# The prompt's attention output computed by token instead of by feature, in a fused prompt and decode step

## The reference, cut to what matters

```
qkv = rms_norm(x) @ w_in                                  # prompt and sample
A) 4 heads, two 64-wide components, 128-wide values:
     w  = softmax(q1 k1^T) - lam * softmax(q2 k2^T)       # causal
     oa = rms_norm(w @ v, subln_g) * (1 - lambda_init)    # norm over each head's 128 values
B) 8 heads x 64, masked softmax:  ob = softmax(q k^T + mask) @ v
x = x + concat(oa, ob) @ w_out
x = x + (silu(h @ w_gate) * (h @ w_up)) @ w_down,  h = rms_norm(x, norm_ffn_g)
y = rms_norm(x, norm_final_g)
```

## Time and profile before

| | |
|---|---|
| median of 3 runs | 1169.67 us (1168.24 to 1173.23) |
| the profiled execution: its own time, its span | 1171.82 us, 1169.7 us |
| mean granted TensorE clock, as a share of full speed | 0.942 |
| busy: PE, PEld, DVE, ACT, POOL | 995.5, 879.7, 568.2, 419.3, 250.3 us |
| attention pieces e0 to e71 | about 332 to 532 us |
| output projection of the prompt | about 535 to 645 us |
| norm and last slots of the sample | about 645 to 742 us |
| feed-forward, final norm | from 742 us |

### The profile page before, as it was taken

The page is one execution under the profiler, slowest core; times in us unless marked ns, Lnnn a source line. Parts: engine busy times, 40 slices in busy tenths (PEclk is TensorE's granted clock), DMA queues, the critical chain, the costliest instruction groups (busy, mean ns, idle before and its releaser), DMA issues.

```text
span 1169.7 us, 29082 instructions
## 1 busy us (share of the span) xinstructions
PE 995.5 (85%) x11290; PEld 879.7 (75%) x11290; DVE 568.2 (49%) x1367; ACT 419.3 (36%) x908; POOL 250.3 (21%) x107
## 2 busy tenths in 40 slices
PE   3978898988878868676887576899999999999994
PEld 3967887777655546454666454899999999999994
DVE  4479747876368999962445252322322322200003
ACT  5553543363126555653413331222222222212112
POOL 2212121211000010102110001333433334433330
PEclk8989999999888998988999788999999999999997
DMA  8589999999899999688986995477676776865632
GB/s 265 209 257 301 327 316 361 361 330 344 308 334 345 350 364 311 211 265 272 318 274 203 265 294 162 164 266 250 233 264 224 263 266 253 296 205 184 217 121 81
DMA packets 202415, 310.90 MB, mean 266 GB/s; under 512 B 14465, under 2 KB 111106, under 8 KB 200770
## 3 DMA queue, kind: packets, MB, share of 16 engines
q1 hardware_dynamic: 200386, 305.24, 77.7%
q10 hardware_dynamic: 1920, 4.20, 1.3%
HBM read 302.30 MB, written 73.92 MB: 322 GB/s over the span
## 4 chain that ended last, share of the span: by engine, by line
PE 51%; DVE 14%; SPq 13%; DMA 10%; issue 7%; ACT 5%; DVEq 0%; ACTq 0%
PE ps L1216 35%; SPq L547 7%; PE ps L897 5%; DMA v_ring<-in_cache_v_diff 4%; DVE kt_sb L1806 3%; SPq L627 3%; PE ps L1085 3%; PE ps L1123 3%; DMA c_raw<-in_w_up 2%; ACT q_st L1476 1%; DVE sub_r L1781 1%; DMA v_ring<-in_state_v_win 1%; DMA g_ffn<-in_norm_ffn_g 1%; DMA k_ring<-in_state_k_win 1%; PE ps L1043 1%
## 5 line engine op out<-in xcount | busy, mean ns | idle before, releaser
L1806 DVE STREAM_TRANSPOSE kt_sb<-k_ring 128x512 f32<-128x512 f32 x336 | 217.5, 686 | 76.7 <-PE ps L1085 31.6
L842 POOL TENSOR_TENSOR c_lo<-c_raw,c_hi 128x1024 fp32r<-128x1024 f32 (+1 forms) x60 | 157.0, 2616 | 364.5 <-ACT c_hi L1529 356.4
L1529 ACT ACTIVATE c_hi<-c_raw 128x1024 fp32r<-128x1024 f32 (+1 forms) x60 | 68.8, 1146 | 316.0 <-PE ps L1216 268.0
L1216 PE MATMUL ps<-h_hi,c_lo 128*128 128x288 f32 x672 | 144.2, 295 | 0.0
L1216 PE MATMUL ps<-h_hi,c_hi 128*128 128x288 f32 x672 | 143.1, 293 | 0.9 <-DVE ffn_tmp L1988 0.9
L1123 PE MATMUL ps<-v_ring,pt_sb 128*32 128x128 f32 (+1 forms) x2496 | 94.0, 296 | 58.0 <-DMA v_ring<-in_cache_v_diff 41.2
L1216 PE MATMUL ps<-h_lo,c_hi 128*128 128x288 f32 x672 | 142.1, 293 | 0.0
L897 PE MATMUL ps<-h_hi,w_hi 128*128 128x288 f32 x384 | 126.1, 328 | 4.4 <-DVE h_lo L1675 2.3
L1123 PEld LDWEIGHTS ps<-v_ring,pt_sb 128*32 128x32 f32 (+1 forms) x2496 | 72.7, 118 | 73.6 <-issue 63.9
L897 PE MATMUL ps<-h_lo,w_hi 128*128 128x288 f32 x384 | 115.7, 301 | 0.0
L897 PE MATMUL ps<-h_hi,w_lo 128*128 128x288 f32 x384 | 115.4, 301 | 0.0
(11 more groups left out here) (172 smaller groups left out, 1587.2 us busy)
## 6 DMA issues: line engine op xcount, KB each, us to landing
k_ring<-in_cache_k_diff SPq DMA_DIRECT2D x256, 256.0 KB, 5.1
v_ring<-in_cache_v_diff SPq DMA_DIRECT2D x256, 256.0 KB, 5.2
out_k_win_sample<-in_state_k_win SPq DMA_DIRECT2D x32, 1020.0 KB, 7.5
out_v_win_sample<-in_state_v_win SPq DMA_DIRECT2D x32, 1020.0 KB, 7.8
k_ring<-in_state_k_win SPq DMA_DIRECT2D x80, 256.0 KB, 5.8
w_raw<-in_w_in SPq DMA_DIRECT2D x24, 512.0 KB, 6.2
c_raw<-in_w_gate SPq DMA_DIRECT2D x22, 512.0 KB, 3.8
c_raw<-in_w_up SPq DMA_DIRECT2D x22, 512.0 KB, 4.2
```

The costliest lines, as they stand in the source:

```text
L842: nc.gpsimd.tensor_tensor(c_lo[:, j, 0:width], c_raw[:, j, 0:width], c_hi[:, j, 0:width].bitcast(F32), ALU.subtract).then_inc(w_lo_done, 1)
L1216: last = nc.tensor.matmul(main_ps[:, 2 * bank + c, 0:HALF], wt[:, j, w], act[:, k0 + k, c * HALF:(c + 1) * HALF], start=start and k == 0 a ...
L1529: nc.scalar.activation(c_hi[:, j, 0:width], c_raw[:, j, 0:width], ACT.Copy).then_inc(w_hi_done, 1)
L1806: V.transpose(kt_sb[:, i, :], k_ring[:, i, :]).then_inc(kt_done, 1)
```

## The change

1. **Output by token.** `weigh` swaps operands: the turned probabilities are the stationary side and the values the moving side, so Y has queries on partitions. For T from 4 each of the two heads moves 64 columns where 128 moved before.
2. **Inverse sums as columns.** For T from 4 the probabilities are no longer scaled: both L1731 instructions go, PE's `turn_weights` waits for ACT's exponentials alone, and DVE's new `evac_out` multiplies Y by the inverse sums (a step-0 operand) while it copies. ACT keeps the copy for T below 4.
3. **Head norm as columns.** The sums of squares are now over the free axis: ACT takes them 128 columns at a time into `head_r` (128x4 a head), DVE's means and inversions and ACT's roots are on 128x4, in three groups (heads 0 and 1, head 2, head 3) where the roots were in two. POOL scales `oT` in four pieces a head, once. The matrix-of-ones products of the prompt go.
4. **Turned back.** PE turns each head's four blocks into bank X (`turn_head`) at e36, e41, ..., e71, after the sample's uses of that step. `mix` reads X one and two pieces later on ACT (which applies g_sub8 for T below 4) and DVE; DVE's part frees X. The output projection takes the tiles in plain order.
5. **Loads.** `g_ffn` has another place and is loaded at o8 (slot 37) after the fourth head's squares. The first chunks of gate and up are issued at slot 45 step 1 instead of slot 48. ACT waits for `scored` before the norm's first squares.

```diff
-        if has_v(t):
-            out.append(("p", t))
...
+            for p in pieces(t, i):
+                if p < OUT and p - ATTN in TURN_AT:
+                    out.append(("h", TURN_AT.index(p - ATTN)))
...
-SQUARES_AT = (19, 27, 35, 43)
-ROOT_AT = (31, 47)
-INVERT_AT = (32, 34, 36, 38, 48, 50, 52, 54)
-HEAD_SCALE_AT = (37, 41, 53, 57)
-MIX_AT = {40: 0, 44: 1, 47: 4, 55: 5, 56: 2, 60: 3, 63: 6, 71: 7}
+SQUARES_AT = (16, 24, 32, 40)
+MEAN_AT, ROOT_AT, INVERT_AT = (27, 36, 43), (29, 38, 45), (31, 40, 47)
+NORMED = ((0, 2), (2, 3), (3, 4))
+HEAD_SCALE_AT = (33, 34, 42, 49)
+TURN_AT = (36, 41, 46, 51, 56, 61, 66, 71)
...
+                if p == OUT + 8:
+                    sp.wait_ge(sub_sq_done, 4)
+                    sp.dma_start(g_ffn[:, :], ins["norm_ffn_g"].partition_broadcast(P)).then_inc(norm_in[1], 16)
...
-                    if (t, i) == (KSLOTS, 1):
-                        sp.wait_ge(scored, KSLOTS)
-                        sp.dma_start(g_ffn[:, :], ins["norm_ffn_g"].partition_broadcast(P)).then_inc(norm_in[1], 16)
-                    if (t, i) == (KSLOTS + 4, 1):
+                    if (t, i) == (KSLOTS + 1, 1):
                         sp.wait_ge(e_t, KT)
                         c_chunk(C_GU, 0, KT, w_gate[:, :, 0:P])
                         c_chunk(C_GU + 1, 1, KT, w_up[:, :, 0:P])
...
             def head_scale(g):
-                r = sub_r[g // 2][:, g % 2, :]
-                pool.wait_ge(sub_rstd, 2 * g + 2)
-                nc.gpsimd.tensor_tensor(r, r, oT[:, g, :], ALU.mult).then_inc(sub_rstd2, 1)
-                pool.wait_ge(sub_rstd2, g + 1)
-                nc.gpsimd.tensor_scalar(oT[:, g, :], r, g_sub8, None, ALU.mult).then_inc(sub_norm, 1)
+                pool.wait_ge(sub_rstd, g + 1)
+                for blk in range(4):
+                    o = oT[:, g, blk * P:(blk + 1) * P]
+                    last = nc.gpsimd.tensor_scalar(o, o, head_r[g][:, blk:blk + 1], None, ALU.mult)
+                last.then_inc(sub_norm, 1)
...
-                pe.wait_ge(weights, u + 1)
+                if u < 16:
+                    pe.wait_ge(weights, u + 1)
+                else:
+                    pe.wait_ge(probs, u + 1)
...
+                        weights_t = probT[:, u % 2, c, kb * P:(kb + 1) * P]
                         if T >= 4:
-                            r = slice(64 * c, 64 * c + 64)
-                            dst, w = Y[r, cols], v_tok[:, kb, T * P + 64 * c:T * P + 64 * c + 64]
+                            last = nc.tensor.matmul(Y[:, qb * P + 64 * c:qb * P + 64 * c + 64], weights_t,
+                                                    v_tok[:, kb, T * P + 64 * c:T * P + 64 * c + 64],
+                                                    start=kb == 0, stop=kb == qb)
...
-            def sum_squares(g):
...
-                nc.tensor.matmul(Z[1], ones[:, :], sub_sq[:, g % 2, :], start=True, stop=True).then_inc(z_full[1], 1)
+            def turn_head(g):
+                if g < 4:
+                    pe.wait_ge(sub_norm, g + 1)
+                else:
+                    pe.wait_ge(y_free, Y_NO["a", g] + 1)
+                pe.wait_ge(x_free, X_NO["h", g])
+                for blk in range(4):
+                    last = nc.tensor.transpose(X[:, blk * P:(blk + 1) * P], oT[:, g, blk * P:(blk + 1) * P], ident[:, :])
+                last.then_inc(x_full, 1)
...
+            def head_squares(g):
+                act.wait_ge(y_free, Y_NO["a", g] + 1)
...
+                for blk in range(4):
+                    last = nc.scalar.activation(head_junk[:, blk, :], oT[:, g, blk * P:(blk + 1) * P], ACT.Square,
+                                                accum_out=head_r[g][:, blk:blk + 1])
...
-                nc.scalar.activation(mix_h[:, g, :], oT[:, g, :], ACT.Copy).then_inc(mix_hi, 1)
+                act.wait_ge(x_full, X_NO["h", g] + 1)
+                nc.scalar.activation(mix_h[:, g, :], X, ACT.Copy, scale=g_sub8 if g < 4 else 1.0).then_inc(mix_hi, 1)
...
+            def evac_out(T):          # on DVE, T from 4
+                dve.wait_ge(pv_done, 4 * T + 4)
+                dve.wait_ge(prd_done, 4 * T + 4)
+                V.tensor_tensor(oT[:, T, :].rearrange("p (k i) -> p k i", i=64), Y.rearrange("p (k i) -> p k i", i=64),
+                                prd[T % 2].unsqueeze(2).to_broadcast([P, 8, 64]), ALU.mult).then_inc(y_free, 1)
...
+            def head_mean(w):
+                for g in range(*NORMED[w]):
+                    dve.wait_ge(sub_sq_done, g + 1)
+                    V.tensor_scalar(head_r[g], head_r[g], 1.0 / P, SUB_EPS, ALU.mult, ALU.add).then_inc(sub_mean, 1)
...
                     if e in INVERT_AT:
-                        w = INVERT_AT.index(e)
-                        r = sub_r[w // 4][:, w // 2 % 2, w % 2 * (SEQ // 2):w % 2 * (SEQ // 2) + SEQ // 2]
-                        dve.wait_ge(sub_rms, w // 4 + 1)
-                        V.reciprocal(r, r).then_inc(sub_rstd, 1)
+                        for g in range(*NORMED[INVERT_AT.index(e)]):
+                            dve.wait_ge(sub_rms, g + 1)
+                            V.reciprocal(head_r[g], head_r[g]).then_inc(sub_rstd, 1)
```

More of the change, by code:

```diff
@@ L220, in x_order @@
     for t in range(SLOTS):
-        if has_v(t):
-            out.append(("p", t))
-        if has_v(t) and is_last(t - LAG):
-            out.append(("m", t))
-        if has_v(t - 1) and is_last(t - 1 - LAG):
-            out.append(("o", item_of(t - 1 - LAG)[0]))
+        for i in range(8):
+            if i == 4 and has_v(t):
+                out.append(("p", t))
+            if i == 6 and has_v(t) and is_last(t - LAG):
+                out.append(("m", t))
+            if i == 6 and has_v(t - 1) and is_last(t - 1 - LAG):
+                out.append(("o", item_of(t - 1 - LAG)[0]))
+            for p in pieces(t, i):
+                if p < OUT and p - ATTN in TURN_AT:
+                    out.append(("h", TURN_AT.index(p - ATTN)))
     return {what: k for k, what in enumerate(out)}
@@ L403, in build @@
         q_st = at("q_st", [P, 2, 4, 4, 32], Q1)
-        g_ffn = at("g_ffn", [P, D], Q1)
+        sq_junk2 = at("sq_junk2", [P, D], Q1)
         q_nat = at("q_nat", [P, 4, 32], region(512))
@@ L441, in build @@
         pden = small[:, 206:214]
[L442 removed]
+        prd = [small[:, 214:222], small[:, 351:359]]
         wide = small[:, 222:254]
@@ L1035, in out_tile @@
                         pe.wait_ge(masked, UNITS)
[L1036 to L1037 removed]
+                for k in (2 * kk, 2 * kk + 1):
                     w = slice(k * P, k * P + P)
                     if m == 0:
[L1040 removed]
+                        pe.wait_ge(x_free, X_NO["h", k] + 1)
                     for wt, act, at_first in ((o_hi[m % 2][:, w], mix_h, True), (o_hi[m % 2][:, w], mix_l, False),
                                               (o_lo[:, m % 2, w], mix_h, False)):
[L1043 to L1044 removed]
+                        last = nc.tensor.matmul(M[m % 2], wt, act[:, k, :], start=k == 0 and at_first,
+                                                stop=k == KT - 1 and act is mix_h and not at_first)
                 if kk == 3:
@@ L1399, in main @@
                         act.wait_ge(e_added, KT)
+                        act.wait_ge(scored, KSLOTS)
                     if r % 2 == 0 and r < 8:
@@ L1409, in main @@
                     m, kk = divmod(p - OUT, 4)
+                    if p == OUT:
+                        mix(KT - 1)
                     if m < KT - 1 and kk == 0:
@@ L1762, in main @@
                     m, kk = divmod(p - OUT, 4)
-                    if p == OUT:
-                        mix(MIXED[-1])
+                    if p == OUT + 1:
+                        mix(KT - 1)
                     if kk == 0 and 2 <= m:
```

101 lines of the change are left out of this document (42 added, 59 removed).

## The result

The changed kernel takes 1164.13 us (median, 1158.21 to 1172.61, 20 runs) where the kernel before, run beside it, took 1171.82 (1166.15 to 1181.72, 20 runs). The ratio is 0.9929, 95% interval [0.9904, 0.9953]: 8.3 us faster, 5.5 to 11.2. The profiled execution took 1161.06 us (span 1159.1), so profile against profile it is 10.8 us. Forecast were 16.5.

A forecast was written before the change was run, and what follows sets the result against it. DVE and DMA were taken as full from 376 to 430, DVE alone to 489, PE from 742. Terms -9 + 0.5 - 8 = -16.5 us from 1171.82 gave 1155.3 (median terms 1153), own range 1149 to 1158, 8 in 10 within 1143 to 1166.

The forecast's parts named there:

- the 8 us of the end: Last slots: early gate and up chunks end ACT's stand and PE's 9.44 us wait, so slot 51 starts 8 us sooner.
- the 9 of the attention: Whole attention: -8 us from 430 to 489, -2 from 489 to 530, +1 for bank X, together -9 us.
- Attention, 430 to 489: DVE does 14 us less there, DMA lets at most 10 go; 8 us taken, of 0 to 14.
- Rival B: DMA binds throughout the attention, which gives only 2 us: 1160 us, chance 0.17.
- rival C: DVE decides and transfers follow: 14 + 4 us in the attention, 9 at the end, 1143 in median terms, chance 0.14.
- Attention, 489 to 530: Removing L1731 there frees 3.62 us of DVE and PE's wait for it: 2 us taken, of 0 to 7.
- PE's products for T from 4: Attention: 160 instructions at 0.10 us each, -8 to +10.6 us, taken as 0; wrong if slower than 0.1 us.
- Turns and bank X: Attention: 32 turns cost PE 5.3 us, hidden in idle time; waits for bank X 0 to 29 us, 1 taken in all.
- Rival D: Slower: eight bank X rounds cost the full 3.67 us each, 29 against 17.5 gained: +12, 1182 us, chance 0.07.
- g_ffn: DVE's 19.83 us stand before the last slots is nearly free; moving the load costs +0.5 us, of -1 to +1.9.
- What follows keeps its length: After slot 51 starts sooner, everything behind it was taken to last as long as before, so the 8 us stay whole.
- Rival E: The end is given back: chunks push the values, PE waits at slots 46 to 49 instead: 1161 us, chance 0.12.

The follow-up runs named there:

- the short inversions: The kernel before with its eight inversions cut from 256 to 8 columns each, so values are not the reference's: 0.9889, and 0.991 when repeated.
- f2: The changed kernel with only the four head-norm heads by token; T from 4 as before, with DVE's scaling, ACT's copy and no turn: 0.9921, 9.3 us.
- e4: The changed kernel with the products for T from 4 back in the old orientation (values stationary, probabilities moving): 0.992.
- g4: The changed kernel with 3 MB more to load into an unread buffer, 1 MB each near slots 32, 34 and 36: 0.9971.
- f1: The changed kernel without its turns into bank X, with mix reading oT itself: 0.9913, 10.2 us.
- e1: The kernel before with only the first gate and up chunks issued early, at slot 45 step 1 instead of slot 48: 0.9975, 2.9 us.
- g2: The kernel before with only the first gate and up chunks issued early, a repeat on another chip: 0.9979, 2.5 us.
- h4: The kernel before with its inversions cut to 8 columns, a repeat with more executions: 0.991, 10.6 us.
- h3: The kernel before with inversions cut to 8 columns and the first gate and up chunks issued early: 0.9902, 11.5 us.
- h2: The kernel before, unchanged, timed against itself and profiled a third time: 0.9966.
- g1: The kernel before with ACT's two splits of the first gate and up chunks moved behind its copy of slot 50's probabilities, loads unmoved: 1.0001.
- e2: The changed kernel with the first gate and up chunks back at slot 48: 0.9944, 6.6 us; its profile is of a slow execution, 1179.03 us.

## Why the prediction was wrong

Direction and range held; the size was twice what was measured on the first pair (16.5 against 8.3), and 4 us too much on the second. The step that failed is the 8 us of the end; the 9 of the attention were too much by 2 to 6 as timed.

- **Attention, 430 to 489: the size right, in part by luck.** Eight us were forecast from what DVE loses there (inversions and L1731), with the DMA share as the cap of 10. Slots 28 to 31 fell from 59.5 to 51.4 in the means, 8.1 us, with the DMA share at 0.93 from 430 to 489. The work named was right only in part: the short inversions, with L1731 kept, take the same slots to 52.0, and f2 to 50.3. Six of the eight inversions lie in these slots, 10.3 us of DVE; with 9.3 us of them gone the slots were 7.5 us shorter, and the rest of what DVE lost did nothing. The place was half wrong: 4.4 of the 8.1 us came in slot 28 (414.38 to 429.39), for whose three inversions the forecast counted nothing because the DMA share was 1.02, and 4.6 in slot 31. The two inversions of slot 32 gave nothing. So some 4 us too much for one stretch and some 4 too little for the other cancel. Rival B (DMA already binds, 2 us) fell; rival C (all 14) fell for this stretch too.
- **Attention, 489 to 530: wrong by its 2 us.** The wait of 3.67 us for L1731's result went as forecast. But slots 32 to 35 became 3.6 us longer, 59.7 to 63.3, all of it in slot 35. e4 (59.9) and f2 (58.5), with the old orientation, point at the products; g4, with the new one, took 59.3. The cause stays open.
- **PE's products for T from 4: wrong premise, hidden.** "With one factor each way I take 0" was +4.6 us in the matmuls (e4), and the forecast's own sign of being wrong, more than 0.1 us a product, came true with 0.144. It was covered as the bound of +10.6 allowed: slots 36 to 43 became 3.6 us shorter, and 32 to 43 sum to 181.7 in both kernels. What ties the sum is not settled: g4 shows the DMA has slack in its first part and little in its second.
- **Turns and bank X: right.** 5.3 us and one wait of 2.5 us between 489 and 545; f1 shows that they cost nothing measurable. Rival D fell.
- **ACT: right.** Table loads took 1.28 us each and the 16 squares 4.7 us where 6.3 were taken. PE's waits for ACT between 430 and 489 are 3.9 us, at 462.0 and 473.6, 10 us and more behind the last table load's end.
- **Whole attention**: 9 forecast, 6.6 and 3.5 timed, 7.6 by the slots (22 to 43: 322.8 to 315.2). What is missing by the slots is less than the 2 us of the term for 489 to 530; the rest of the difference is within the noise of the timed runs.
- **g_ffn: +0.5 forecast, nothing measured.** DVE's wait of 19.83 us went. e1 and g2, which kept it, end as soon (79.9 and 79.0 us to `product`) as the changed kernel (81.3 and 78.1): it was nearly free, as the forecast said.
- **The end: the step that failed.** "PE's 9.44 us of standing before 711.83 go ... So slot 51 starts at about 711 - 1.9 = 709 instead of 716.94: -8 us". In the profiled pair this came as worked out. PE's values of slot 51 began 62.8 us after slot 43's scores before (716.94) and 54.9 us after them in the changed kernel, 7.9 us sooner:

```profile
702.86 1.08 PE L1130 MATMUL ps<-v_ring,pt_sb 64*32 64x128 f32 x32 [0.68 <-ACT pt_sb L1508]
```

The whole stretch to `product` was 6.4 us shorter (87.7 to 81.3). But timed, the chunks gave 2.9, 2.5 and 0.9 us (e1, g2, h4 to h3), and in the two other profiles of the kernel before slot 51 began 57.9 and 57.6 us after slot 43 with nothing changed. The term was mis-sized since it was read from an execution in which that stand was 10.69 us; in another of the same kernel it was 1.08 (h2), and on average it costs PE 3.6. g1 says that even this is not on the path alone: with the stand gone and the loads left in place, nothing was gained that could be measured.
- **"What follows keeps its length": wrong by some 3.5 us in the profiled pair.** The first half of gate and up took from 720.7 to 740.8 before, 20.1 us, and from 706.6 to 728.2 after, 21.6. In windows of the changed kernel the granted clock is 1.00 (2.4 GHz throughout) from 700 to 706 and 0.72 in the next six us (part of them at 1.2 GHz), with matmuls of 0.44 us among those of 0.29:

```profile
700.00:706.00 6.00, 4.67 (x129) 3.37 (x118) 0.62 (x3) 0.86 (x2) 0.00 (x0) 1.00 0.05 14
706.00:712.00 6.00, 5.46 (x27) 5.01 (x29) 2.69 (x5) 0.00 (x0) 2.38 (x1) 0.72 1.02 307
```

In the kernel before the lower clock came a little earlier, beside the sample's last products, and was over when the first half began:

```profile
712.00:720.00 8.00, 7.01 (x149) 5.48 (x145) 0.17 (x1) 0.86 (x2) 0.51 (x1) 0.76 0.01 2
720.00:726.00 6.00, 5.38 (x35) 4.07 (x37) 2.77 (x5) 0.00 (x0) 2.38 (x1) 1.00 1.00 309
```

Between gate and down PE stood 1.95 us for POOL's low part where it had not stood before. Both differ from one execution to the next (the first half: 20.0 to 24.9 us over all profiles, 20.1, 21.5 and 24.9 in the three of the kernel before), so they belong to the pair, not to the change. Rival E (the end is given back) is borne out in size, not in mechanism: PE's waits for values in the last slots did not grow, 6.0 us in the changed kernel and 8.6 before. Its cause, chunks that push the values, shows only as the issue of the up chunk, which held SP's queue for 6.20 us, with the next values behind it; whether that delay costs time was not tried alone.

```profile
661.12 0.53 SPq L608 DMA_DIRECT2D c_raw<-in_w_gate  x1
...
661.70 6.20 SPq L608 DMA_DIRECT2D c_raw<-in_w_up  x1
667.94 5.68 SPq L549 DMA_DIRECT2D v_ring<-in_state_v_win  x2
```

**What stays open.** Profiles put the early chunks at 6.4 us (means of 7 and 9, which scatter by 3.6 and 1.7), timed runs at 1 to 3 with intervals of about 3.5 each. Of the 6.4 us, 3.6 are PE's waits for ACT's copies, and 2.6 are PE's own busy time on the same matmuls (means of 63.0 and 60.4 us, at a granted clock of 0.78 and 0.81). Without e2 it is 3.1 and 2.2 of 5.4. Whether late chunks make PE's own work dearer was not tried. The 3 to 4 us of waits fit both the profiles and the timed runs. It stays open why slots 32 to 43 add to 180 to 185 us in every kernel but g4, and why the changed attention ends later than the short inversions while the chunks are late.

On the rule of the Trainium skill that the forecast weighed (ScalarE: Activation LUTs, "What ACT_TABLE_LOAD costs"): no wait of PE stands at the further load or at the one back here, and ACT's work after the load began at 407.9 where the load began at 406.6, 1.3 us, as in the earlier trace rows; the drain of 1.38 us beside the load doesn't show.

## What to carry to other kernels

Before a wait seen in a profile is priced, look at the same wait in a second and third execution: a stand that depends on when a transfer lands was 10.69 us in one and 1.08 in another, and only its mean can be won. Where several engines are full in turn, find the one edit that frees the fullest of them (here eight inversions, by making them 128x4) and value the others at what the next resource leaves; here everything in the attention after the first 8 us was worth nothing measurable. When a wait is taken out of one profile, look also at what the work around it cost in that profile: here the execution with the longest wait had the cheapest matmuls. Time a null pair, the same kernel against itself, before a term of 3 us is believed.

## What the runs showed of the hardware

- An fp32 product with 64 moving columns and a 128-wide stationary side is no cheaper than one with 128 moving columns and a 64-wide one: 16 instructions took 1.90 us (0.119 each) with a 128x128 stationary side and 64 columns moved, against 1.58 us (0.099) with a 128x64 stationary side and 128 moved. The weight loads rose from 158 to 219 ns.
- An inversion of 128x8 takes 0.16 us, of 128x256 1.71.
- POOL's scaling of 128x128 by a column takes 0.60 us.
- The issue of a 512 KB load held SP's queue for 6.20 us while others were outstanding, the one before it for 0.53.
- The same 800 matmuls of the last slots and the first half kept PE busy for 56.4, 60.8 and 66.6 us in three executions of one kernel, at a mean granted clock of 0.84, 0.80 and 0.73.
